# Two seven-product feed-forward passes: down slabs loaded ahead of the hand-over, entry sums on GpSimd, first operand in halves

## The reference, cut to what matters

```python
def swiglu(h, w_gu, w_d):
    g, u = jnp.split(h @ w_gu, 2, axis=-1)
    return (jax.nn.silu(g) * u) @ w_d
...
x = x + 0.5 * mx[2] * swiglu(modulate(rms_norm(x, norm_g[i, 0]), mx[0], mx[1]), ffn1_w_gu[i], ffn1_w_d[i])
x = x + mx[5] * fourier_mix(hx, fourier_w[f])
x = x + 0.5 * mx[8] * swiglu(modulate(rms_norm(x, norm_g[i, 2]), mx[6], mx[7]), ffn2_w_gu[i], ffn2_w_d[i])
```

## Time and profile before

| | us |
|---|---|
| median of 3 runs | 3035.6 |
| lowest and highest of them | 3032.35 and 3040.41 |
| the profiled execution | 3029.0 |
| its span on the core | 3027.1 |

### The profile page before, as it was taken

How to read it: one execution, slowest core, us unless ns; L and a number is a source line. 1 busy time by engine, 2 the same in 40 slices (tenths; PEclk the granted TensorE clock), 3 DMA queues, 4 the chain that set the end, 5 groups by cost and what they waited for, 6 DMA issues and landing times.

```text
span 3027.1 us, 42365 instructions
## 1 busy us (share of the span) xinstructions
PE 2877.9 (95%) x16662; PEld 2321.2 (77%) x16662; DVE 1676.8 (55%) x2926; ACT 1077.3 (36%) x1963; POOL 266.0 (9%) x302
## 2 busy tenths in 40 slices
PE   8999999999989999998999898999899988999995
PEld 7888888877846888887999798999788865874442
DVE  5646343545587564667877668877532277521113
ACT  4112111232175322225544446545333266321111
POOL 1000000001100100000000030000010155012221
PEclk9999999999999999999999999999999999999998
DMA  7232323311000365552322222322222200448985
GB/s 290 98 132 100 130 103 127 96 68 56 29 1 17 139 242 194 208 182 96 118 94 100 96 79 70 107 103 105 77 89 96 104 29 1 186 155 356 368 354 232
DMA packets 84792, 395.60 MB, mean 131 GB/s; under 512 B 17808, under 2 KB 22288, under 8 KB 57872
## 3 DMA queue, kind: packets, MB, share of 16 engines
q1 hardware_dynamic: 73104, 384.87, 34.3%
q0 software_dynamic: 11520, 8.43, 0.9%
HBM read 443.56 MB, written 16.78 MB: 152 GB/s over the span
## 4 chain that ended last, share of the span: by engine, by line
PE 86%; DVE 7%; ACT 2%; DMA 2%; issue 1%; POOL 1%; SPq 0%; DVEq 0%; ACTq 0%; POOLq 0%
PE ps L910 9%; PE ps L911 9%; PE ps L912 9%; PE ps L3707 5%; PE ps L1374 5%; PE ps L1376 5%; PE ps L1375 5%; PE ps L3729 3%; PE ps L1392 3%; PE ps L1393 3%; PE ps L1394 3%; PE ps L2741 2%; PE ps L2742 2%; PE ps L2743 2%; PE ps L2098 2%
## 5 line engine op out<-in xcount | busy, mean ns | idle before, releaser
L1374 PE MATMUL ps<-x_high_ffn,weights_high_ffn 128*128 128x256 f32 x1232 | 353.7, 287 | 24.7 <-DVE x_low_ffn L1568 18.7
L910 PE MATMUL ps<-h_high_ffn,weights_high_ffn 128*128 128x512 f32 (+1 forms) x1024 | 361.4, 353 | 0.2 <-DVE weights_low_ffn L1071 0.2
L911 PE MATMUL ps<-h_low_ffn,weights_high_ffn 128*128 128x512 f32 (+1 forms) x1024 | 361.5, 353 | 0.0
L912 PE MATMUL ps<-h_high_ffn,weights_low_ffn 128*128 128x512 f32 (+1 forms) x1024 | 361.0, 353 | 0.0
L1375 PE MATMUL ps<-x_low_ffn,weights_high_ffn 128*128 128x256 f32 x1232 | 353.0, 286 | 0.0
L1376 PE MATMUL ps<-x_high_ffn,weights_low_ffn 128*128 128x256 f32 x1232 | 352.8, 286 | 0.0
L1374 PEld LDWEIGHTS ps<-x_high_ffn,weights_high_ffn 128*128 128x128 f32 x1232 | 240.7, 195 | 29.2 <-issue 19.7
L1375 PEld LDWEIGHTS ps<-x_low_ffn,weights_high_ffn 128*128 128x128 f32 x1232 | 240.9, 196 | 2.5
L1376 PEld LDWEIGHTS ps<-x_high_ffn,weights_low_ffn 128*128 128x128 f32 x1232 | 240.7, 195 | 0.0
L910 PEld LDWEIGHTS ps<-h_high_ffn,weights_high_ffn 128*128 128x128 f32 x1024 | 193.7, 189 | 27.4 <-issue 0.6
L911 PEld LDWEIGHTS ps<-h_low_ffn,weights_high_ffn 128*128 128x128 f32 x1024 | 193.7, 189 | 26.2
(11 more groups left out here) (529 smaller groups left out, 6165.8 us busy)
## 6 DMA issues: line engine op xcount, KB each, us to landing
weights<-in_ffn_gu SPq DMA_DIRECT2D x88, 1024.0 KB, 5.1
big<-in_w_exp_gu SPq DMA_DIRECT2D x32, 2048.0 KB, 13.0
scratch_ffn<-in_w_mod SPq DMA_DIRECT2D x35, 1536.0 KB, 6.5
down_raw_ffn<-in_ffn_d SPq DMA_DIRECT2D x40, 512.0 KB, 5.7
weights<-in_w_in SPq DMA_DIRECT2D x16, 1024.0 KB, 4.9
weights<-in_w_exp_dn SPq DMA_DIRECT2D x15, 1024.0 KB, 19.1
hbuf<-in_w_exp_dn SPq DMA_DIRECT2D x12, 1024.0 KB, 19.2
scratch_ffn<-in_w_mod SPq DMA_DIRECT2D x11, 1024.0 KB, 5.0
```

Of the source, the lines that this page charges most:

```text
L910: pe.matmul(out, wh, xh, start=(k == 0), stop=False)
L911: pe.matmul(out, wh, xl, start=False, stop=False)
L912: mm = pe.matmul(out, wl, xh, start=False, stop=(k == n - 1))
L1374: pe.matmul(out, wh, xh, start=(fresh and k == 0), stop=False, skip_group_check=True)
```

## The change

1. **Hand-over.** In `ready` both hand-overs get the sort key `last_of[-1] + AHEAD - 2`, which is 186 + 8 - 2 = 192, in place of 174 and 186. The order on SP becomes: raw 19, raw 20, raw 21, hand-over 0, hand-over 1, raw 22, raw 23.
2. **Entry sums.** The five weight sums of step -1 (slab 0: 5, 7, 6; slab 1: 5, 7) are issued by GpSimd, behind its wait for the stage before (`follows`). All later sums stay with DVE.
3. **First operand in two pieces.** ACT makes `x_high` of operand 1 after two `x_shift` for the contraction tiles 0 and 1 and again after two more for tiles 2 and 3; DVE makes `x_low` of the first piece after five `scale` and of the second after the other three. PE waits for the first piece at item 0 and for the second ahead of tile 2 of item 0.
4. **Order.** `low(4)` goes ahead of `turn(5)`.

```diff
-        made_x = (1, 2, 7, 6, 4, 5, 3)
+        made_x = ((1, 0), (1, 1), 2, 7, 6, 4, 5, 3)
...
-                ready += [(used_last["gate_up", max(r for r in range(KF) if r % 3 == s)], 2, s) for s in range(2)]
+                ready += [(last_of[-1] + AHEAD - 2, 2, s) for s in range(2)]
...
-                        wait(pe, "x_low", made_x.index(which) + 1)
+                        wait(pe, "x_low", 1 if which == 1 else made_x.index(which) + 1)
...
                     for k in range(KH):
+                        if n == 0 and k == 2:
+                            wait(pe, "x_low", 2)
...
+                    if which in ((1, 0), (1, 1)):
+                        at = slice(2 * which[1], 2 * which[1] + 2)
+                        wait(scalar, "shifted", at.stop)
+                        signal(scalar.activation(X_high[:, 0, at, :], plain(0, 0)[:, at, :], ACT.Copy), "x_high")
+                        return
...
-                for k in range(KH):
-                    x_shift(k, 0)
-                x_high(1)
+                x_shift(0, 0)
+                x_shift(1, 0)
+                x_high((1, 0))
+                x_shift(2, 0)
+                x_shift(3, 0)
+                x_high((1, 1))
...
             def _(gpsimd):
                 follows(gpsimd, prior)
+                for g, which in sorted(sum_at[-1], key=lambda p: (p[0], SUM_ORDER.index(p[1]))):
+                    weight_sum(gpsimd, g, which)
...
                 low(0)
                 invert_roots(vector, NX)
                 low(1)
-                sums_of(-1)
                 vector.wait_ge(nm["spread"].sem, s0 + 1)
-                for k in range(KD):
+                for k in range(KH + 1):
                     scale(k, 0)
-                x_low(1)
+                x_low((1, 0))
+                for k in range(KH + 1, KD):
+                    scale(k, 0)
+                x_low((1, 1))
...
                 turn(7)
+                low(4)
                 turn(5)
-                low(4)
```

More of the change, by code:

```diff
@@ L1302, in plain, with weight_sum @@
             return full[:, k_half * KH:(k_half + 1) * KH, t_half * HALF:(t_half + 1) * HALF]
-        made_x = (1, 2, 7, 6, 4, 5, 3)
+        made_x = ((1, 0), (1, 1), 2, 7, 6, 4, 5, 3)
         sources = {1: plain(0, 0), 2: plain(1, 0), 3: plain(1, 1), 7: T[:, 0], 6: T[:, 1], 4: T[:, 2], 5: T[:, 3]}
+        def weight_sum(eng, g, which):
+            buf = ring.buf[:, g % 3, :]
+            a11, a12, a21, a22 = (buf[:, j * Q:(j + 1) * Q] for j in range(4))
+            s1, s2 = S[:, g % 2, 0, :], S[:, g % 2, 1, :]
+            if which == 5:
+                eng.wait_ge(ring.landed[g % 3], 16 * landing(g))
+                if g > 1:
+                    wait(eng, "low", item_at[g - 2, 5] + 1)
+                ins = eng.tensor_tensor(s1, a21, a22, ALU.add)
+            elif which == 7:
+                wait(eng, "sums", summed[g, 5])
+                ins = eng.tensor_tensor(a21, a21, a11, ALU.subtract)
+            elif which == 6:
+                wait(eng, "sums", summed[g, 7])
+                if g > 1:
+                    wait(eng, "low", item_at[g - 2, 6] + 1)
+                ins = eng.tensor_tensor(s2, s1, a11, ALU.subtract)
+            else:
+                wait(eng, "sums", summed[g, 6])
+                wait(eng, "low", item_at[g, 1] + 1)
+                ins = eng.tensor_tensor(a11, a12, s2, ALU.subtract)
+            signal(ins, "sums")
         prior = list(ended)
@@ L1448, in x_high @@
                 def x_high(which):
-                    if which in (1, 2, 3):
-                        wait(scalar, "shifted", {1: KH, 2: KD, 3: 2 * KD}[which])
+                    if which in ((1, 0), (1, 1)):
[3 more added lines that the diff above has]
+                        return
+                    if which in (2, 3):
+                        wait(scalar, "shifted", {2: KD, 3: 2 * KD}[which])
                     else:
@@ L1512, in low, with sums_of @@
                     signal(vector.tensor_tensor(out, src, w.bitcast(F32), ALU.subtract), "low")
[L1514 to L1540, removed]
+                def sums_of(e, first=0, end=None):
+                    for g, which in sorted(sum_at.get(e, ()), key=lambda p: (p[0], SUM_ORDER.index(p[1])))[first:end]:
+                        weight_sum(vector, g, which)
                 def join(e):
@@ L1567, in x_low @@
                     wait(vector, "x_high", made_x.index(which) + 1)
+                    if which in ((1, 0), (1, 1)):
+                        at = slice(2 * which[1], 2 * which[1] + 2)
+                        signal(vector.tensor_tensor(X_low[:, 0, at, :], plain(0, 0)[:, at, :],
+                                                    X_high[:, 0, at, :].bitcast(F32), ALU.subtract), "x_low")
+                        return
                     signal(vector.tensor_tensor(X_low[:, which - 1], sources[which],
@@ L1587, in settled @@
                     if tail is not None:
-                        gained_low(vector, tail, m, base["x_high"] + 7)
+                        gained_low(vector, tail, m, base["x_high"] + len(made_x))
                 low(0)
@@ L1647, in feed_forward_seven @@
                      "joined": len(joins), "silued": 2 * KF, "multiplied": KF, "hidden_high": KF, "hidden_low": KF,
-                     "scaled": 2 * KD, "shifted": 2 * KD, "turned": 4, "x_high": 7, "x_low": 7, "added": n_down}[n]
+                     "scaled": 2 * KD, "shifted": 2 * KD, "turned": 4, "x_high": len(made_x), "x_low": len(made_x), "added": n_down}[n]
         for b, c in enumerate(down_landed):
```

## The result

The changed kernel took 3003.7 us (median of 4 runs, 2998.38 to 3004.99) against 3035.44 us before (4 runs, 3032.35 to 3040.41): a ratio of 0.9891 with a 95% interval of 0.9873 to 0.9908, or 28 to 39 us less. The profiled execution is the one of 3004.99 us, its span 3003.0 us.

A forecast was written before the change was run, and what follows sets the result against it. DVE was taken to bound each pass's entry, PE the middle, and a latency chain behind a late down slab the end. Ends 26.3 plus entries 3.3 gave 29.6 us: 3035.6 - 29.6 = 3006, range 2996 to 3017.

The forecast's parts named there:

- The hand-over: Ends of both passes: down loads issued ahead of the hand-overs remove PE's idle gap and slow restart, 14.8 + 11.5 = 26.3 us.
- the slab's landing: Pass end: a 512 KB down slab lands in at or below 5.7 us after issue, 7.7 as the bad end.
- A: Rival, pass ends: slabs land in 7.7 us, raw 20 1 us late; about 2 us lost per pass, 3010; chance 0.11.
- E: Rival, slower: raw 22 and 23 behind the 2 MB stall PE at items 198 and 200; 3054; chance 0.02.
- The restart at the slow clock: Behind each pass-end gap: PE's first matmuls no longer run slowly, gain 2.4 us in pass 1, 1.4 in pass 2.
- The sums: Entries: moving five sums from DVE to GpSimd brings `scale` 2.6 us earlier per pass; net entry gains 2.1 and 1.2.
- the lock: Entries: GpSimd instructions hold up DVE ones with both operands in SBUF; 0.45 us lost in pass 1, 1.3 in pass 2.
- C: Rival, entries: PE, not DVE, sets the pace from item 0; 9 us gained for both entries, 3000; chance 0.08.
- the pieces: Entries: making the first operand in two pieces adds one DVE instruction, costing 0.06 us.
- B: Rival, entries: three DVE instructions each wait for a whole GpSimd one; 1.3 us lost per entry, 3012; chance 0.10.
- the clock behind the entry: Middle of the passes: a slower clock giving back the time saved at the ends would prove the prediction wrong; no size given.

The follow-up runs named there:

- e1: The kernel before with the new hand-over keys alone: 3006.5 us (4 runs), 0.9906 of the kernel before beside it.
- e11: The changed kernel itself, timed once more beside later variants: 3003.5 us (4 runs), 0.990 of the kernel before beside it.

## Why the prediction was right

The forecast was 3006 (2996 to 3017), 29.6 us less; the medians differ by 31.7. By its steps:

- **The hand-over** (26.3 us forecast): right in place, cause and size. Item 188 stands 3.15 us behind item 187 where 3.4 was forecast, so 12.63 and 10.43 us went against 12.4 and 10.1, and e1 as a whole gained 26.0. SP waits 3.0 us, forecast 4. The step that was most uncertain, the slab's landing, was too careful: raw 19 to 21 took 3.6, 4.2 and 3.4 us, 5.7 was taken; so A fell. Raw 22, now the one behind the 2 MB, took 7.3 us and landed at 1728.04, 2.4 us ahead of `high(198)` at 1730.47, where 2 us of cover were forecast: no new wait, so E fell. What the text did not see is that 2.4 us of the 12.63 were DVE held up by GpSimd; the sum took the old gap as measured, so its size did not suffer.
- **The restart at the slow clock** (2.4 and 1.4 of those): right. Counted from item 188, the matmuls of the changed kernel come 2.3 us sooner than before in pass 1, of which 1.95 reach pass 2, and 1.3 us sooner in pass 2. Later jumps of the clock cover that in e1's tail.
- **The sums** (2.6 us a pass, less the lock): DVE sets the pace, as said, and C fell: PE starts item 0 4.4 and 3.3 us sooner and item 11 only 2.38 and 1.30 us sooner. Forecast were 2.1 and 1.2. Inside that sum two terms were off and cancelled in part: in pass 1 no time was lost to the lock where 0.45 stood, because the last sum ended before `x_low` began; in pass 2 it was 1.1 where 1.3 stood; and the pieces cost 0.2 where 0.06 stood, a term that no row gave (`x_low` takes 1.23 us in one and 0.69 twice in pieces, 0.15 more). B had the mechanism right and its size wrong: two of DVE's instructions were held up in pass 1 and three in pass 2, but those of pass 1 lay in DVE's slack ahead of the roots.
- **What the sum left out:** the clock behind the entry. The text named it among the things that would make it wrong, with no price. It took 1.5 us in pass 2 of the changed kernel, so that pass came to item 187 no sooner than before (327.33 against 327.14 us), and pass 1 in e11. It doesn't come from the new entry: e1 has it with the old one. Whether the earlier down loads make it more frequent is open.
- **The two profiled executions** differ by only 24.1 us of span. The parts are 12.63 + 10.43 for the hand-overs, 2.38 - 0.19 for the ways to item 187, 1.95 between the passes, 2.47 in the tail, and 5.53 against it ahead of pass 1, in code that is the same. Without these 5.53 us the parts come to 29.7, the forecast's 29.6; so close a match is partly luck, since the 1.5 us of slow clock that the sum lacks are nearly made good by the tail: of its 2.47 us the restart explains 1.3 and nothing in the sum the rest. The forecast made against the median and not against the low profiled execution of before was the better one for this reason.

## What to carry to other kernels

A queue that waits in order is read by asking what stands behind each wait and what it will need: here one sort key put a hand-over and 2 MB ahead of half a megabyte that ACT takes 5.4 us after its buffer is free. Late issue and what is fetched ahead are two costs, 5.1 and 7.5 us of the same stall, and can be priced apart; and a load that lands early also starts its consumer early, here a GpSimd instruction that held DVE for 2.4 of the 7.5 us. Where one engine sets the pace of a start-up, work taken from it counts up to its next wait (sums of 3.4 us gave 2.6 and 1.5), and an earlier start of the engine that it feeds counts for nothing.

## What the runs showed of the hardware

- One 128 x 512 sum takes 1.27 us on GpSimd and 0.69 on DVE. Beside each other, a DVE instruction with two SBUF operands takes up to 1.68 and one of GpSimd up to 1.71, each held until the other is done; beside two GpSimd instructions of 128 x 1024 (2.35 and 2.79 us) two such DVE instructions took 3.69 us instead of 1.29. With a PSUM operand DVE isn't held (0.41 us each).
- A 512 KB load landed in 3.4 to 4.2 us (raw 19 to 21) with no larger load just ahead, and in 7.3 right behind 2 MB (raw 22), against 5.7 and 7.7.
- Clock losses come in steps: 1.5 us behind an entry, and up to some 11 in a tail whose code is unchanged. At the entries short pauses of PE avoid them (six of six passes with fillers); for the tail the cause was not tested. They move the whole kernel by as much as a small edit does: medians of four runs could not tell 1 us.
